# Inverting the triangular matrices of a delta-rule recurrence with 64x64 instead of 32x32 products, with read-out and preparation rearranged

## The chip, the cores and the metric

One core of one Trainium2 chip runs the whole program. The metric is device time in microseconds (us) of one execution; fewer is better.

## The reference

The program is a multi-block network on 512 latent and 256 context tokens. The change touches its recurrent mixer (twelve heads of 64, two directions), here cut to that:

```python
def rwkv_prepare(p, mu, w0, w2, a0, a2, g2, k_k, k_a):
    ...
    logw = -jax.nn.softplus(-(w0 + jnp.einsum('btdr,drc->btdc', jnp.tanh(wd), w2)).astype(f32)) - 0.5
    decay = jnp.exp(-jnp.exp(logw))
    a = jax.nn.sigmoid((a0 + jnp.einsum('btdr,drc->btdc', ad, a2)).astype(f32))
    g = jax.nn.sigmoid(gd) @ g2
    kk = (k * k_k).reshape(B, T, H_A, RWKV_HEAD)
    kk = kk / jnp.maximum(jnp.linalg.norm(kk, axis=-1, keepdims=True), 1e-12)
    kd = k[:, :, None, :] * (1.0 + (a - 1.0) * k_a)
    bd = kk.reshape(B, T, 1, D_A) * a
    ...
def wkv_scan(S0, r, w, k, v, kk, b, reverse):
    def step(S, inp):
        r_t, w_t, k_t, v_t, kk_t, b_t = inp
        sa = -jnp.einsum('bhij,bhj->bhi', S, kk_t)
        S = S * w_t[:, :, None, :] + sa[..., :, None] * b_t[:, :, None, :] + v_t[..., :, None] * k_t[:, :, None, :]
        return S, jnp.einsum('bhij,bhj->bhi', S, r_t)
    ...
def rwkv_readout(y, r, v, kd, g, r_k, lnx_g, lnx_b):
    mu = y.mean(-1, keepdims=True)
    var = jnp.mean(jnp.square(y - mu), -1, keepdims=True)
    yn = ((y - mu) * lax.rsqrt(var + GN_EPS)).reshape(B, T, D_A) * lnx_g + lnx_b
    coef = jnp.sum(r[:, :, None] * kd * r_k, axis=(2, 4))
    bonus = (coef[..., None] * v).reshape(B, T, D_A)
    return ((yn + bonus) * g).astype(g.dtype)
```

## The kernel before

The program is some twenty stages in a row; most multiply by streamed weights. The stage `rwkv_pairs` (L2240) runs the recurrence. It works on six pairs of heads (`PAIRS`), two heads filling the 128 partitions, and cuts the 768 tokens into twelve chunks (`NCH`) of 64 (`RC`). Within a chunk the recurrence is solved by the inverse of a 64x64 triangular matrix, made from products of keys; from chunk to chunk a 64x64 state is carried. The stage before it (`lora`, L1951) makes the inputs `wd`, `ad`, `gd` of the low-rank products.

Each engine has its instructions in the order in which they are written, and engines meet at semaphores. For `i` from -1 to 6 every engine runs `advance(i)`, then `recur(i)`:

- `advance(i)`, the *inversion phase*, does three jobs, interleaved by hand: it inverts the matrices of pair `i`, prepares pair `j = i+1`, and reads out pair `e = i-1`.
- `recur(i)`, the *recurrence phase*, takes twelve steps, each for both directions. It also makes the triangular matrices of pair `j` in twelve *units* (`turn_unit`, `triangle_unit`, and `triangles` on DVE), one to a step from the third step on, and the last two behind the steps. Before pair 0 the units stand alone: with the first preparation they make the stage's prologue.

**Inverting.** The matrices come in four groups (`COMBOS`: two directions, six chunks each). A 64x64 matrix is inverted by doubling: level 0 is identity minus the part next to the diagonal (POOL), levels 1 to 4 take the two diagonal 32-blocks up to their full size, and the join (`join_first`, `join_second`) adds the block between them. A level `l` of a group is a chain over four engines: POOL masks the matrix into `ct` (two buffers by `l % 2`); PE multiplies it by the inverse so far (`g_products`, L2403); ACT copies the product out of PSUM (`copy_g`, L2634); PE multiplies again (`u_products`, L2412); DVE subtracts that from `x` (`inverse`, L2808) and transposes it into `xd` (`turn_over`, L2802). Products are made by 32x32 quadrants of PE (`QUADS`), so that a 32-block is a matrix of its own; that is why `triangles` copies the diagonal 32-blocks once more, into `own` (L2929), and why the finished blocks and the join go into `xt`, by eight ACT copies (`copy_diagonal`, L2643) and eight on DVE (`join`).

**Preparing.** Per direction: `lora_decay` and `lora_rate`, fp32 products of 64 rows (L2378, `wide`); sigmoids (L2610, L2617); a scan and its centring (L2745); `linear_rate` (L2622) and `exponentials` (L2625, L2627); products for rates, query, receptance and updates on DVE. Each change between sigmoid and exponential loads a table on ACT.

**Reading.** `copy_y` (L2648), `mean` (PE, L2378 with `bones`), `centre_y` (DVE), `square_y` (L2652), `variance`, `root_y` (L2656), `invert_root` (L2826), `spread_root` (L2091), `scale_y` (L2830), `affine_y`, then `coefficients`, `bonus`, `add_bonus`, `gate` and `gate_y`. Before a recurrence starts to add up its outputs in PSUM, PE fills that area with zeros by a product (L2540).

## Time and profile before

| | before |
|---|---|
| median of 3 runs | 4580.6 us (4576.47 to 4582.39) |
| profiled execution | 4571.39 us, its span 4569.6 us |
| PE busy | 3924.0 us (86%) |
| PE weight loads | 3194.7 us (70%) |
| DVE busy | 1340.0 us (29%) |
| ACT busy | 1303.4 us (29%) |
| POOL busy | 1187.6 us (26%) |
| instructions | 86006 |

Busy times are shares of the span of the one profiled execution; engines overlap. The stage `rwkv_pairs` lies between about 2204 and 2962 us of that span: the prologue until 2276, then inversion and recurrence phases in turn, and at the end the read-out of the last pair. In the trace an fp32 product of PE is two records (an fp32r product is one), so a count there is twice the count of products in the code.

### The profile page before, as it was taken

Reading aid. Unit: us, or ns where it says so; the run is one execution under the profiler, and the core shown is the slowest. Engines: PE = TensorE matmul, PEld = TensorE weight load, DVE = VectorE, ACT = ScalarE, POOL = GpSimd, SP = SyncE. Lnnn points to the kernel's source line nnn. Section 1 sums busy time; section 2 is a strip of 40 time slices with the busy share of each in tenths; the row PEclk is TensorE's granted clock in tenths of the full one; section 3 lists DMA queues with packets and bytes.
Section 4 is the critical chain, followed back from the end, with each engine's and each line's share of the span. In section 5 each row is a group of like instructions: output and inputs, shape, how many; then the busy total and the mean of one; then the engine's idle time right before and its main releaser. Section 6 shows DMA issues by size and latency. Waiting matters only on the chain. (4 is left out here: it accounts for less than half of the span.)

```text
span 4569.6 us, 86006 instructions
## 1 busy us (share of the span) xinstructions
PE 3924.0 (86%) x36748; PEld 3194.7 (70%) x36748; DVE 1340.0 (29%) x2838; ACT 1303.4 (29%) x2196; POOL 1187.6 (26%) x665
## 2 busy tenths in 40 slices
PE   6798699999798899769588787678999969997997
PEld 4676588888576677658466666567888848765885
DVE  1327211111344211155455555331111130352111
ACT  0315321111354322232233333222112132453222
POOL 0311222222233333222111100112222213453442
PEclk8899899999899899989777777699999989998999
DMA  7210132232200435222200000003323202111221
...
DMA packets 120335, 343.82 MB, mean 75 GB/s; under 512 B 35551, under 2 KB 41567, under 8 KB 119647
## 3 DMA queue, kind: packets, MB, share of 16 engines
...
q14 instruction: 67, 0.55, 0.0%
...
## 5 line engine op out<-in xcount | busy, mean ns | idle before, releaser
L204 POOL TENSOR_TENSOR feed_low<-ring,feed_high 128x1024 fp32r<-128x1024 f32 (+1 forms) x240 | 626.8, 2612 | 1310.8 <-ACT feed_high L197 1310.8
L221 PE MATMUL ps<-hn_high,feed_high 128*128 128x512 f32 (+1 forms) x2112 | 758.1, 359 | 129.4 <-POOL feed_low L204 124.3
L221 PE MATMUL ps<-hn_low,feed_high 128*128 128x512 f32 (+1 forms) x2112 | 751.6, 356 | 0.0
L221 PE MATMUL ps<-hn_high,feed_low 128*128 128x512 f32 (+1 forms) x2112 | 750.5, 355 | 0.0
L221 PEld LDWEIGHTS ps<-hn_high,feed_high 128*128 128x128 f32 x2112 | 401.6, 190 | 214.9 <-issue 151.8
L221 PEld LDWEIGHTS ps<-hn_high,feed_low 128*128 128x128 f32 x2112 | 401.1, 190 | 56.8
L221 PEld LDWEIGHTS ps<-hn_low,feed_high 128*128 128x128 f32 x2112 | 401.8, 190 | 55.1
L197 ACT ACTIVATE feed_high<-ring 128x1024 fp32r<-128x1024 f32 (+1 forms) x240 | 272.9, 1138 | 487.3 <-PE ps L221 485.9
L1089 DVE TENSOR_TENSOR ps<-feed_gate,ps 128x768 f32<-128x768 f32 (+1 forms) x88 | 73.0, 830 | 1077.5 <-PE ps L221 1077.5
L221 PE MATMUL ps<-feed_hid_high,feed_high 128*128 128x512 f32 (+1 forms) x1056 | 377.6, 358 | 5.3 <-DVE feed_hid_low L1092 5.3
L221 PE MATMUL ps<-feed_hid_low,feed_high 128*128 128x512 f32 (+1 forms) x1056 | 377.2, 357 | 0.0
L221 PE MATMUL ps<-feed_hid_high,feed_low 128*128 128x512 f32 (+1 forms) x1056 | 376.5, 356 | 0.0
L221 PEld LDWEIGHTS ps<-feed_hid_high,feed_high 128*128 128x128 f32 x1056 | 201.7, 191 | 34.7 <-issue 6.1
L221 PEld LDWEIGHTS ps<-feed_hid_high,feed_low 128*128 128x128 f32 x1056 | 201.6, 191 | 28.6
L221 PEld LDWEIGHTS ps<-feed_hid_low,feed_high 128*128 128x128 f32 x1056 | 201.5, 191 | 28.0
L1052 ACT ACTIVATE feed_hid_high<-ps 128x768 f32 (+3 forms) x88 | 62.1, 705 | 551.1 <-DVE ps L1089 551.1
L1058 ACT ACTIVATE feed_gate<-ps 128x768 f32<-128x768 f32 (+1 forms) x88 | 62.0, 705 | 497.1 <-PE ps L221 497.1
L951 DVE SCALAR_TENSOR_TENSOR h<-ps,mod_even,h 128x512 f32 x96 | 54.8, 613 | 453.6 <-PE ps L221 453.6
L221 PE MATMUL ps<-project_mixed_high,project_high 128*128 128x512 f32 (+1 forms) x384 | 141.4, 368 | 26.6 <-DVE project_mixed_low L935 26.6
L2361 POOL TENSOR_TENSOR rwkv_ct<-rwkv_own,rwkv_level_mask 128x192 f32<-128x192 f32 x24 | 14.2, 592 | 520.5 <-DVE rwkv_own L2929 520.5
L204 POOL TENSOR_TENSOR project_low<-ring,project_high 128x1024 fp32r<-128x1024 f32 x32 | 78.5, 2455 | 243.8 <-ACT project_high L197 243.7
L221 PE MATMUL ps<-project_mixed_low,project_high 128*128 128x512 f32 (+1 forms) x384 | 140.0, 365 | 0.0
...
## 6 DMA issues: line engine op xcount, KB each, us to landing
...
```

Of the source, the lines that this page charges most:

```text
L197: act.activation(self.high[:, j % self.slots, 0:w], feed.ring[:, slot, 0:w], ACT.Copy).then_inc(self.high_ready, 1)
L204: pool.tensor_tensor(self.low[:, j % self.slots, 0:w], feed.ring[:, slot, 0:w], self.high[:, j % self.slots, 0:w].bitcast(F32), ALU.subtra ...
L221: mm = pe.matmul(dst, weights[a], values[b], start=first and n == 0, stop=last and n == 2)
L951: ins = dve.scalar_tensor_tensor(out=hs, in0=region(k, r)[:, a:b], scalar=k.mod[:, bass.ds(n + gate_at * KC, 1), s], in1=hs, op0=ALU.mult, ...
L1052: act.activation(hid[0][:, bass.ds(n, 1), :].rearrange("p a t -> p (a t)"), whole, ACT.Copy).then_inc(hid_high_ready, 1)
L1058: act.activation(gate, GATE, ACT.Silu).then_inc(gated, 1)
L1089: dve.tensor_tensor(whole, gate, UPR, ALU.mult).then_inc(multiplied, 1)
L2361: pool.tensor_tensor(ct[:, d, 0, gs, :], own[:, d, gs, :], levels[:, d, 0, :].unsqueeze(1).to_broadcast([P, GR, 32]), ALU.mult)
```

## The change

- **Levels.** A level now takes both 32-blocks of a 64x64 matrix in one product: weights of 64 columns and 32 streamed ones on two halves of PE, in place of 32 and 16 on four quadrants. POOL masks the full 64x64 matrix straight from `lt`, with one buffer `ct`, so a mask waits for the product that last read it. `own` and `xt` go; the join writes into `xd`, half of it on ACT and half on DVE. Level 0 of groups 0 and 1 and the level-1 masks of these are made in the recurrence before; groups 2 and 3 have their level 0 on DVE, at the start of `advance`.
- **Centring.** The values are multiplied by identity minus 1/64 as they are turned, so that outputs come out centred; `mean` and `centre_y` go.
- **Low-rank products** take split operands: high and low parts in fp32r, three products in place of one fp32 product. The `lora` stage makes `wide_high` and `wide_low`; ACT and POOL split the weights of the next pair in the recurrence. The reciprocal root is split likewise for `spread_root`, and the zero fill is an fp32r product.
- **Sigmoid** is 0.5 tanh(0.5 x + 0.5 b) + 0.5: a tanh and a scaled copy.
- **GpSimd** takes `rates` and `add_bonus` from DVE. The stage's constants come by fewer DMAs.
- The order within `advance` is another on every engine.

```diff
     act.activation(gd, gd, ACT.Sigmoid)
+    act.drain()
+    act.activation(wide_high[:, 0, :], wd, ACT.Copy).then_inc(high_ready, 1)
...
+    for n, m in enumerate((1, 0)):
+        dve.wait_ge(high_ready, n + 1)
+        dve.tensor_tensor(wide_low[:, m, :], inputs[:, m, :], wide_high[:, m, :].bitcast(F32), ALU.subtract)
...
-    for dst, name in ((ident2, "ident2"), (lmask, "tri_mask")):
-        sp.dma_start(dst[:], k.io[name]).then_inc(S["constants"], 16)
-    for q, qs in enumerate(QUADS):
-        cols = slice(32 * (q % 2), 32 * (q % 2) + 32)
-        sp.dma_start(ident32[qs, :], k.io["ident2"][qs, cols]).then_inc(S["constants"], 16)
-        sp.dma_start(levels[qs, :, :, :], k.io["level_mask"][qs, :, 0:JOIN, cols]).then_inc(S["constants"], 16)
+    sp.dma_start(ident2[:], k.io["ident2"]).then_inc(S["constants"], 16)
+    sp.dma_start(lmask[:, :, :], k.io["tri_mask"][:, :, 0:2 * RC]).then_inc(S["constants"], 16)
+    sp.dma_start(levels[:, :, :, :], k.io["level_mask"][:, :, 0:JOIN, :]).then_inc(S["constants"], 16)
...
+    def level_mask(i, l, c):
+        d, gs = COMBOS[c]
+        if l == 1 and c > 1:
+            pool.wait_ge(S["x_ready"], 20 * i + c + 1)
+        if l > 1:
+            pool.wait_ge(S["g_done"], 20 * i + 4 * (l - 2) + c + 1)
+        return pool.tensor_tensor(ct[:, d, gs, :], lt[d][:, gs, 0, :],
+                                  levels[:, d, l, :].unsqueeze(1).to_broadcast([P, GR, RC]), ALU.mult)
+
+    def rates(j, d):
+        pool.wait_ge(S["lin_ready"], 2 * j + d + 1)
+        pool.wait_ge(S["landed"], 48 * (j + 1))
+        if d == 0:
+            if j > 0:
+                pool.wait_ge(S["prep_done"], j)
+            pool.tensor_tensor(chunked(kds[:, j % 3, :]), decay, chunked(key), ALU.mult).then_inc(S["decay_free"], 1)
+        else:
+            pool.tensor_tensor(decay, decay, chunked(key), ALU.mult)
+        pool.tensor_tensor(a, a, unit, ALU.mult).then_inc(S["rates_done"], 1)
...
+            rates(j, 0)
+        if inverting:
+            for l in (3, 4):
+                for c in range(4):
...
+                if i >= 0:
+                    pool.wait_ge(S["sa_done"], 24 * i + 12)
+                pool.wait_ge(S["lt_ready"], 12 * j + 4 + c + 1)
+                level_mask(j, 0, c)
+                pool.drain()
+                pool.tensor_tensor(xd[:, d, gs, :], ident2[:, :].unsqueeze(1).to_broadcast([P, GR, RC]), ct[:, d, gs, :],
+                                   ALU.subtract).then_inc(S["xd_first"], 1)
             pool.drain()
...
+            for c in range(2):
+                level_mask(j, 1, c).then_inc(S["ct_ready"], 1)
...
-    def wide(dst, weights, src):
+    def wide(dst, parts):
+
         for a_, b_, _ in spans(TOK):
-            mm = pe.matmul(dst[:, a_:b_], weights, src[:, a_:b_], start=True, stop=True)
+            for n, (weights, values) in enumerate(parts):
+                mm = pe.matmul(dst[:, a_:b_], weights, values[:, a_:b_], start=n == 0, stop=n == len(parts) - 1)
...
+    def low_rank(dst, high, low, rows, m):
+        return wide(dst, ((high, wide_high[rows, m, :]), (high, wide_low[rows, m, :]), (low, wide_high[rows, m, :])))
...
+            for hs in HALVES:
+                mm = pe.matmul(k.ps[hs, c, 32 * m:32 * m + 32].rearrange("p (b w) -> p b w", w=2 ** l),
+                               ct[hs, d, n, :], one(x[hs, d, n, :], l, d), start=True, stop=True)
...
+            for hs in HALVES:
+                mm = pe.matmul(k.ps[hs, c, 32 * (GR + m):32 * (GR + m) + 32], xd[hs, d, n, :], g[hs, d, n, :],
                                start=True, stop=True)
...
-    def variance(e):
-        pe.wait_ge(S["ysq_ready"], e + 1)
         sums.quarters(pe, 4, t1).then_inc(S["var_done"], 1)
...
+        for q in range(4):
+            dst = k.ps[:, 4 + q // 2, QT * (q % 2):QT * (q % 2 + 1)]
+            pe.matmul(dst, pick_r[:, q, :], root_high[:, :], start=True, stop=False)
+            mm = pe.matmul(dst, pick_r[:, q, :], root_low[:, :], start=False, stop=True)
...
         if preparing:
             lora_decay(j, 0)
-        if reading:
-            mean(e)
         for l in range(1, JOIN):
             if inverting:
-                for c in range(4):
-                    g_products(i, l, c)
+                g_products(i, l, 0)
+                g_products(i, l, 1)
+            if reading and l == 1:
+                variance(e)
+            if inverting:
+                g_products(i, l, 2)
+                g_products(i, l, 3)
+            if preparing and l == 1:
+                lora_rate(j, 0)
+            if preparing and l == 3:
+                lora_decay(j, 1)
+            if reading and l == 4:
...
-                mm = pe.matmul(k.ps[hs, 7, m * RC:(m + 1) * RC], val[hs, j % 2, n * RC:(n + 1) * RC], ident2[hs, :],
+                mm = pe.matmul(k.ps[hs, 7, m * RC:(m + 1) * RC], val[hs, j % 2, n * RC:(n + 1) * RC], centre2[hs, :],
...
-                pe.matmul(R2[:, a_:b_], zeros[:, :], wd[:, a_:b_], start=True, stop=False)
+                pe.matmul(R2[:, a_:b_], blank[:, :], wide_high[:, 0, a_:b_], start=True, stop=False)
...
+        act.activation(decay, chunked(R3), ACT.Tanh, scale=0.5, bias=half_bias(j, d))
+        act.drain()
+        act.activation(decay, decay, ACT.Copy, scale=0.5, bias=0.5).then_inc(S["decay_ready"], 1)
+
...
-        act.activation(a, R3, ACT.Sigmoid, bias=p(j, f"a0_{d}")).then_inc(S["a_ready"], 1)
+        act.activation(a, R3, ACT.Tanh, scale=0.5, bias=half_bias(j, 2 + d)).then_inc(S["a_ready"], 1)
...
+        act.drain()
+        act.activation(a, a, ACT.Copy, scale=0.5, bias=0.5)
...
-    def copy_diagonal(i, d):
-        for q, qs in enumerate(QUADS):
-            ins = act.activation(xt[qs, d, :, 32 * (q % 2):32 * (q % 2) + 32], xd[qs, d, :, :], ACT.Copy)
-        ins.then_inc(S["xt_diagonal"], 1)
...
+    def join(i, c):
+        d, gs = COMBOS[c]
+        act.wait_ge(S["u_done"], 20 * i + 16 + c + 1)
+        for h in range(2):
+            qs = QUADS[2 * h + d]
+            ins = act.activation(xd[qs, d, gs, 32 - 32 * d:64 - 32 * d], k.ps[qs, c, GR * 32:GR * 64].rearrange("p (n c) -> p n c", c=32),
+                                 ACT.Copy, scale=-1.0)
+        ins.then_inc(S["join_odd"], 1)
...
+    def square_y(e):
         act.wait_ge(S["y_done"], e + 1)
+        act.activation(t1[:, :], R2, ACT.Square)
         act.activation(k.mo[:, e, :], R2, ACT.Copy).then_inc(S["y_copied"], 1)
...
-    def rates(j, d):
-        dve.wait_ge(S["lin_ready"], 2 * j + d + 1)
-        dve.wait_ge(S["landed"], 48 * (j + 1))
...
+    def first_level(i, c):
         d, gs = COMBOS[c]
...
+        dve.tensor_tensor(ct[:, d, gs, :], lt[d][:, gs, 0, :], levels[:, d, 0, :].unsqueeze(1).to_broadcast([P, GR, RC]), ALU.mult)
+        dve.drain()
+        dve.tensor_tensor(xd[:, d, gs, :], ident2[:, :].unsqueeze(1).to_broadcast([P, GR, RC]), ct[:, d, gs, :], ALU.subtract)
...
-        dve.tensor_tensor(xs, xs, packed(k.ps[:, c, GR * 16:GR * 32], l), ALU.subtract)
-        turn_over(i, l, c)
+        dve.tensor_tensor(xs, xs, packed(k.ps[:, c, GR * 32:GR * 64], l), ALU.subtract)
+        dve.drain()
+        dve.transpose(flat(xd[:, d, gs, :]), flat(x[:, d, gs, :])).then_inc(S["x_ready"], 1)
...
-    def centre_y(e):
-        dve.wait_ge(S["mean_done"], e + 1)
-        dve.scalar_tensor_tensor(out=k.mo[:, e, :], in0=R2, scalar=-1.0 / HEAD, in1=k.mo[:, e, :],
-                                 op0=ALU.mult, op1=ALU.add).then_inc(S["centred"], 1)
...
-        dve.reciprocal(root[:, :], root[:, :]).then_inc(S["rec_ready"], 1)
+        dve.reciprocal(root[:, :], root[:, :])
+        dve.drain()
+        dve.tensor_scalar(root_high[:, :], root[:, :], 1.0, None, ALU.mult)
+        dve.drain()
+        dve.tensor_tensor(root_low[:, :], root[:, :], root_high[:, :].bitcast(F32), ALU.subtract).then_inc(S["rec_ready"], 1)
...
-        for q, qs in enumerate(QUADS):
-            cols = slice(32 * (q % 2), 32 * (q % 2) + 32)
-            ins = dve.tensor_tensor(own[qs, d, 2 * u:2 * u + 2, :], k.ps[qs, 6, :].rearrange("p (n w) -> p n w", n=2)[:, :, cols],
-                                    lmask[qs, d, cols].unsqueeze(1).to_broadcast([32, 2, 32]), ALU.mult)
-        ins.then_inc(S["lt_ready"], 1)
+        dve.tensor_tensor(lt[d][:, 2 * u:2 * u + 2, :, :].rearrange("p n j c -> p (n j c)").rearrange("p (m w) -> p m w", m=4),
+                          k.ps[:, 6, :].rearrange("p (m w) -> p m w", m=4),
+                          lmask[:, d, :].unsqueeze(1).to_broadcast([P, 4, 2 * RC]), ALU.mult).then_inc(S["lt_ready"], 1)
```

PE in `advance(1)` (inverting pair 1, preparing pair 2, reading pair 0), from the first low-rank product to the second products of level 1. Before:

```order
L2378 MATMUL ps<-lora,rwkv_lora_weights 128x512
L2378 MATMUL ps<-lora,rwkv_lora_weights 128x256
L2378 MATMUL ps<-mo,rwkv_bones 128x512
L2378 MATMUL ps<-mo,rwkv_bones 128x256
L2403 MATMUL ps<-rwkv_x,rwkv_ct 32x16 x96
L2412 MATMUL ps<-rwkv_g,rwkv_xd 32x16 x48
```

And now:

```order
L2447 MATMUL ps<-lora_high,rwkv_wa_high 128x512
L2447 MATMUL ps<-lora_low,rwkv_wa_high 128x512
L2447 MATMUL ps<-lora_high,rwkv_wa_low 128x512
L2447 MATMUL ps<-lora_high,rwkv_wa_high 128x256
L2447 MATMUL ps<-lora_low,rwkv_wa_high 128x256
L2447 MATMUL ps<-lora_high,rwkv_wa_low 128x256
L2475 MATMUL ps<-rwkv_x,rwkv_ct 64x32 x24
L2094 MATMUL ps<-rwkv_t,rwkv_bones 32x192 x4
L2475 MATMUL ps<-rwkv_x,rwkv_ct 64x32 x24
```

The mean product is gone, the variance moved up between the groups of level 1, and a level's first product is 48 instructions in place of 96.

POOL for one pair. Before:

```order
L2361 TENSOR_TENSOR rwkv_ct<-rwkv_own,rwkv_level_mask 128x192
L2364 TENSOR_TENSOR rwkv_xd<-rwkv_ident,rwkv_ct 128x192
L2371 TENSOR_TENSOR rwkv_ct<-rwkv_own,rwkv_level_mask 128x192 x16
L2361 TENSOR_TENSOR rwkv_ct<-rwkv_own,rwkv_level_mask 128x192
L2364 TENSOR_TENSOR rwkv_xd<-rwkv_ident,rwkv_ct 128x192
```

The first two rows come four times before the third, which is four levels of four masks; the last two begin the next pair. And now:

```order
L2377 TENSOR_TENSOR rwkv_ct<-h,rwkv_level_masks 128x384
L2426 TENSOR_TENSOR rwkv_xd<-rwkv_ident,rwkv_ct 128x384
L2377 TENSOR_TENSOR rwkv_ct<-h,rwkv_level_masks 128x384
L2426 TENSOR_TENSOR rwkv_xd<-rwkv_ident,rwkv_ct 128x384
L2377 TENSOR_TENSOR rwkv_ct<-h,rwkv_level_masks 128x384 x2
L2369 TENSOR_TENSOR rwkv_wa_low<-rwkv_lora_weights,rwkv_wa_high 128x256
L2377 TENSOR_TENSOR rwkv_ct<-h,rwkv_level_masks 128x384 x6
L2386 TENSOR_TENSOR rwkv_kds<-ring 128x768
L2389 TENSOR_TENSOR ring<-ring 128x768
L2377 TENSOR_TENSOR rwkv_ct<-h,rwkv_level_masks 128x384 x8
L2388 TENSOR_TENSOR ring<-ring 128x12x64
L2389 TENSOR_TENSOR ring<-ring 128x768
```

The masks have twice the columns (`h` is the memory of `lt`), and the products for the rates (L2386 to L2389) stand among them, two of the four ahead of the masks of levels 3 and 4. The first six rows are now reached within the recurrence before.

## Rows read from the trace of the kernel before

**Rows 1.** Stretches: length, busy of PE, PEld, DVE, ACT, POOL, clock, DMA, GB/s

```profile
2276.00:2330.60 54.60, 41.47 (x1750) 32.10 (x1750) 28.03 (x64) 21.31 (x41) 13.81 (x18) 0.50 0.03 5
...
2378.50:2448.90 70.40, 51.40 (x1778) 36.18 (x1778) 33.46 (x69) 24.88 (x45) 11.64 (x18) 0.55 0.09 16
2448.90:2497.20 48.30, 43.57 (x1185) 41.42 (x1185) 32.19 (x113) 15.96 (x64) 3.55 (x7) 0.99 0.10 31
2855.80:2913.80 58.00, 37.40 (x1756) 30.02 (x1756) 19.89 (x55) 12.96 (x32) 10.15 (x18) 0.59 0.02 4
2942.00:2961.00 19.00, 10.87 (x28) 5.61 (x28) 6.13 (x6) 3.04 (x4) 0.00 (x0) 0.66 0.00 0
```

**Rows 2.** Timeline of PE in the inversion phase of pair 1: start, length, operation

```profile
2389.44 2.93 PE L2378 MATMUL ps<-lora,rwkv_lora_weights 64*128 64x512 f32 x4
...
2406.44 2.92 PE L2091 MATMUL ps<-rwkv_root,rwkv_pick 128*128 128x192 f32 x8 [2.23 <-DVE rwkv_root L2826]
...
2412.15 2.75 PE L2403 MATMUL ps<-rwkv_x,rwkv_ct 32*32 32x16 f32 x192
2414.73 0.90 PE L2412 MATMUL ps<-rwkv_g,rwkv_xd 32*32 32x16 f32 x50
...
2445.99 2.93 PE L2540 MATMUL ps<-lora,rwkv_zeros 128*128 128x512 f32 x4
```

**Rows 3.** Timeline of PE in the prologue, 64x64 products

```profile
2243.64 0.45 PE L2516 MATMUL ps<-rwkv_ident,rwkv_bb 64*64 64x64 f32 x4
2243.85 0.45 PE L2516 MATMUL ps<-rwkv_ident,rwkv_kb 64*64 64x64 f32 x4
...
2247.30 0.28 PE L2516 MATMUL ps<-rwkv_ident,rwkv_kb 64*64 64x64 f32 x4
2247.42 0.28 PE L2516 MATMUL ps<-rwkv_ident,rwkv_bb 64*64 64x64 f32 x4
```

**Rows 4.** Timeline of PE in the stage before, fp32r products

```profile
2000.15 0.39 PE L221 MATMUL ps<-hn_low,lora_high 128*128 128x512 f32 x1
2000.37 0.39 PE L221 MATMUL ps<-hn_high,lora_low 128*128 128x512 f32 x1
```

**Rows 5.** Groups of DVE by shape, 2277 to 2960: busy, mean ns, idle before

```profile
L2802 DVE STREAM_TRANSPOSE rwkv_xd<-rwkv_x 128x192 f32<-128x192 f32 x96 | 36.3, 379 | 7.3
L2808 DVE TENSOR_TENSOR rwkv_x<-rwkv_x,ps 128x96 f32<-128x96 f32 x96 | 23.7, 247 | 178.6 <-PE ps L2412 178.5
L2745 DVE TENSOR_TENSOR_SCAN ring<-rwkv_within,ring 128x780 f32<-128x780 f32 x10 | 18.9, 1893 | 11.3 <-ACT ring L2610 10.8
...
L2830 DVE TENSOR_TENSOR mo<-mo,ps 128x768 f32<-128x768 f32 x6 | 5.5, 923 | 3.0 <-PE ps L2091 3.0
```

**Rows 6.** Groups of POOL by shape: masks of levels, and a 768-column subtraction elsewhere

```profile
L2371 POOL TENSOR_TENSOR rwkv_ct<-rwkv_own,rwkv_level_mask 128x192 f32<-128x192 f32 x96 | 63.5, 689 | 52.8 <-PE ps L2403 51.2 <-issue 1.0
...
L649 POOL TENSOR_TENSOR hn_low<-affine_whole,hn_high 128x768 fp32r<-128x768 f32 x12 | 21.7, 1812 | 182.8 <-ACT hn_high L645 182.8
```

**Rows 7.** Groups of ACT by shape, 2277 to 2960

```profile
L2643 ACT ACTIVATE rwkv_xt<-rwkv_xd 32x384 f32<-32x384 f32 x48 | 24.9, 518 | 0.6
L2625 ACT ACT_TABLE_LOAD x10 | 12.8, 1283 | 0.2
```

**Rows 8.** Stretches for PE alone: busy, clock, DMA share, GB/s

```profile
2242.00:2244.00 2.00, 2.00 (x28) 0.50 0.04 8
2250.00:2252.00 2.00, 0.84 (x24) 1.00 0.83 299
2290.00:2292.00 2.00, 2.00 (x165) 0.50 0.03 8
```

**Rows 9.** Timeline of DVE, last units of pair 1's recurrence

```profile
2490.17 0.69 DVE L2924 TENSOR_TENSOR h<-ps,rwkv_tri_mask 128x512 f32<-128x512 f32 x1 [1.25 <-PE ps L2528]
2490.78 0.91 DVE L2929 TENSOR_TENSOR rwkv_own<-ps,rwkv_tri_mask 32x64 f32<-32x64 f32 x4
2492.88 0.69 DVE L2924 TENSOR_TENSOR h<-ps,rwkv_tri_mask 128x512 f32<-128x512 f32 x1 [1.19 <-PE ps L2528]
```

350 lines of the change are left out of this document (183 added, 167 removed).

## The prediction

> **What bounds the kernel now.** I read the views from the outside in. The page's first part makes TensorE (PE) the busy engine, but its share is an average over twenty stages. The change touches one of them, the recurrent stage (`rwkv_pairs`), and prepares its inputs one stage earlier. So I cut that stage with the stretches view [rows 1]. Each of the six head pairs passes an *inversion phase* (PE, VectorE (DVE), ScalarE (ACT) and GpSimd (POOL) take turns) and a *recurrence phase* of twelve steps. A full inversion phase takes 70.4 us and PE is busy for 51.4 us of it; a recurrence takes 48.3 us, PE busy for 43.6. The granted clock differs just as much: 0.55 against 0.99, so the inversion phase runs mostly at TensorE's lower level, 1.2 GHz, and the recurrence at 2.4 GHz. Neither phase is bound by one engine's throughput. The timeline of the inversion phase shows PE going from group to group [rows 2] with holes of 1.5 to 4 us, in which ACT copies a product out of PSUM or DVE subtracts and transposes.
>
> **The change, part by part.** All of it is costed against the profiled execution: 4571.4 us, span 4569.6, which is 9.2 us under the median 4580.6.
>
> *PE, level products.* Of each of four levels, 192 + 192 quadrant instructions, counted as the records of the trace (32 weight columns, 16 streamed), become 96 + 96 half instructions (64 weight columns, 32 streamed). At the lower clock the quadrant group takes 2414.73 - 2412.15 = 2.58 us for 192, 13.4 ns each [rows 2]; four quadrants run side by side, so one takes 54 ns. A half product with 64 weight columns and 64 streamed takes 0.21/4 = 53 ns at 1.2 GHz and 0.12/4 = 29 ns at 2.4 GHz [rows 3]; two halves run side by side, so one takes 106 ns. A quadrant product costs half of that: it follows the weight columns (32 of 64), not the streamed ones (16 of 64). So I price a new one by its 64 weight columns: 96 x 53 ns = 5.1 us per group at 1.2 GHz, 96 x 29 ns = 2.8 us at 2.4 GHz. The other bound, streamed columns alone, is half of each. Eight groups: 40.8 us or 22.3 us, against about 19 us in the phase before. At an equal clock the PE loses here.
> The Trainium skill ("TensorE: Matmul & The Clock Gate", section "LDWEIGHTS") gives a weight load as P/1.2 ns, P being columns; that is 53 ns for 64 columns and 27 ns for each of two side by side, at either clock. By it the low-clock group would take 2.6 us, and all of the low-clock case below would fall onto the high-clock one. The row of the 1.2 GHz product, 53 ns for each of two, does not agree, so I keep the row.
>
> *PE, wide products.* The four low-rank products go from fp32 at 2.9 us (1.2 GHz) [rows 2] to three fp32r passes. At 2.4 GHz such a pass takes 0.22 us for 512 columns [rows 4], 0.33 for the 768 here, so three are 1.0 us, and 2.0 at 1.2 GHz. The mean product (2.9) goes. Spreading the root falls from 2.9 to 1.3, the zero fill before the recurrence from 2.9 to 0.7. Coefficients and gate stay (2.9 each).
>
> *PE, sum of an inversion phase.* At 1.2 GHz: 40.8 + 4 x 2.0 + 5.8 + 0.8 (variance) + 1.3 + 4.1 (join) + 0.7 = 61.5 us. At 2.4 GHz: 32.8.
>
> *DVE.* A level step was 0.25 + 0.38 us, 0.64 from one to the next [rows 5]. Twice the columns at about 1 ns each (from 96 to 768 columns an operation goes from 0.25 to 0.92 [rows 5]) make 0.94; 16 of them are 15.0. First level: four operations of 0.54 and two transposes, 3.4. Scans 3.8 [rows 5], centring 2.0, root with its split 2.0, scale, bonus and gate 2.8, query to updates 4.1, half of the join 1.5: 34.6 us busy. GpSimd takes over 3.7 us of rates, and its masks double from 0.69 us to between 1.0 and 1.4 each [rows 6].
>
> *ACT.* Two of four table loads of 1.28 us per phase go [rows 7], and so do the eight copies into `xt` (0.52 us each [rows 7]); two 0.85 us copies come in behind each tanh pair. They lie beside PE work, except the copies before the join.
>
> *What the path becomes.* If the clock were high throughout, PE's 32.8 us would lie under a chain that DVE sets: its 34.6 us plus what it waits where a level's last product must cross PE. These waits are 2.5 before the first level, 1.6 after it, 0.3 at the second scan, 3.8 behind gate and rate product before level 4, 1.4 at the join and 1.8 for handoffs: 11.4, in all **46 us**. If it stayed low, PE is the chain: 61.5 and 2.5 for handoffs, **64 us**. Which one? In the windows of the prologue [rows 8], half products alone took the clock from 0.50 to 1.00 and kept it there while PE was busy for only 0.84 us of 2. The quadrant products of today sit at 0.50 with PE full. The new phase has half products everywhere, but still holes of about 2 us (behind the root, before level 4). I take 53 us, some 60% of the way from low to high.
>
> *Sum, against 4571.4.* Pairs 1 to 4: 70.4 or a little more, to 53, four times 17.4 = 69.6 saved. Pair 0 (54.6 us, no reading part): bounds 38 and 56, 45 taken, 9.5 saved. Pair 5 (58.0, nothing prepared): bounds 35 and 56, 43 taken, 15 saved. Triangles: four small DVE operations (0.91 us) leave each unit. Inside a recurrence that is free, since DVE idles there; in the last units of each, 2.71 us apart because PE waits for DVE [rows 9], it is on the path: 2.3 x 5 = 11.5. The prologue has twelve such units, 10 us, and 2.5 us in its chain of preparation, where four table loads (5.1) leave and tanh copies, weight split and GpSimd rates (0.9 us slower per operation [rows 5, 6]) enter. Last readout [rows 1]: mean and centring out, root split in, 3. The stage before gains two ACT and two DVE operations, which lie beside the pooling chain: 0. Together 121 us, giving 4450 for the profiled execution, 9.2 more for the median: **4460 us**.
>
> **The rivals.**
> 1. *Clock high throughout.* For: the prologue's windows. Against: holes of 2 us, after which today's phase is always back at 0.50. Savings 12.5 + 16.6 + 4 x 24.4 + 23 + 11.5 + 3 = 164; median 4416. Chance 0.15.
> 2. *Clock low throughout the inversion.* Then pair 0 loses 1.4, pairs 1 to 4 gain 6.4 each, pair 5 gains 2: 12.5 - 1.4 + 25.6 + 2 + 11.5 + 3 = 53; median 4527. Chance 0.10.
> 3. *GpSimd becomes the wait.* `ct` has one buffer now, so the mask of a level starts when the last level's first product is done, and the level-3 masks stand behind two rates of 1.81 us that wait for ACT. At 1.4 us a mask, four masks per level are 5.6 us where a level of my chain has 9 to 12; only the rates push, some 5 us a pair. That gives 58 a phase, median 4485. Chance 0.08. The Trainium skill ("GPSIMD Engine Reference", section "Engine selection") says elementwise work with two inputs belongs on VectorE, being about twice as slow here; 1.81 against 0.92 us agrees.
> 4. *Slower: the recurrence loses its clock.* Today the 2.9 us zero fill runs right before each recurrence [rows 2], and the clock is up when the steps begin. The change cuts it to 0.7 us. If 64-column products could not lift the clock by themselves, 43.6 us of busy PE would double: five recurrences 35 us longer each and the last 25, 200 us lost against 121 gained, median 4660. It decides when the low clock lasts for over 0.6 of every recurrence. Against it: the prologue lifts the clock on just such products [rows 8]. Chance 0.05, with mixed forms of it.
> 5. *DVE and GpSimd slow each other* until the gain is eaten. Today a 192-column mask takes 0.69 us on average with DVE busy beside it and 1.81 us is the price of 768 columns [rows 6], about what size alone explains, so little is lost there. No change then; chance 0.02.
>
> **How the numbers follow.** Forecast 0.60, rivals as above; 4460 is the likeliest case, a phase of 53 us, own range 4440 to 4490. The range runs from rival 1 to rival 2: 4415 to 4527, leaving out the slower cases and the tails. A difference under 0.2% (9 us) cannot be told from none by this measurement. Faster is the sum of the forecast and rivals 1 to 3, 0.93; the same is rival 5, 0.02; slower is rival 4, 0.05.
>
> **What would show it.** In the stretches of the changed kernel: phases of pairs 1 to 4 at 48 to 58 us with a granted clock of 0.7 to 0.85; half groups of 24 instructions at 29 or 53 ns each, at 15 or 27 ns if I have mispriced weight columns (then another 10 to 20 us less at the low clock, all in all); recurrences still 46 to 49 us at 0.99; DVE about 34 us busy in a phase, GpSimd 25 to 30; the last units of a recurrence 1.8 us apart. I am wrong if the phase is above 60 us, if `ct` on GpSimd is what PE waits for most, or if a recurrence shows a clock under 0.9.

## The result and the profile after

The changed kernel takes **4496.9 us** (median of 4 runs, 4495.9 to 4509.1), beside 4578.5 us for the kernel before: a ratio of 0.983, with a 95% interval of 0.981 to 0.986. It is faster by 1.7%, some 80 us. The forecast was 4460 us (4415 to 4527), faster: the sign and the range hold, but a third of the forecast gain is missing (the profiled executions differ by 74.7 us; the sum said 121).

The page of the changed kernel, its span and its busy times:

```profile
span 4494.9 us, 76585 instructions
PE 3964.1 (88%) x32152; PEld 3289.1 (73%) x32152; DVE 1318.6 (29%) x2530; ACT 1291.9 (29%) x2185; POOL 1288.9 (29%) x677
```

Nine thousand instructions fewer, and PE busy 40 us *more* in a span 75 us shorter. The stretches view of the changed kernel, cut at the end of the last triangle and at the first product of a recurrence (stretch, length, busy of PE, PEld, DVE, ACT, POOL, clock, DMA share, GB/s): inversion phase of pair 0; phase and recurrence of pair 1; phases of pairs 4 and 5:

```profile
2265.60:2321.80 56.20, 53.80 (x986) 50.93 (x986) 32.60 (x58) 19.55 (x38) 24.78 (x18) 0.53 0.04 7
...
2368.30:2426.10 57.80, 53.57 (x1010) 47.48 (x1011) 36.45 (x63) 23.02 (x42) 25.53 (x19) 0.68 0.07 14
2426.10:2473.30 47.20, 44.86 (x1185) 42.71 (x1184) 25.56 (x65) 15.74 (x65) 6.79 (x7) 0.96 0.14 37
...
2684.70:2742.90 58.20, 56.05 (x1010) 49.62 (x1011) 36.49 (x64) 23.13 (x42) 25.52 (x19) 0.63 0.03 9
2790.30:2840.00 49.70, 46.04 (x963) 41.90 (x959) 24.85 (x53) 10.47 (x27) 15.54 (x15) 0.65 0.01 3
```

A full phase fell from 72 to 58 us. The same cut in the kernel before, which leaves the last unit's copies into `own` in the phase, gives 71.3, 72.9, 72.8 and 72.3 us for pairs 1 to 4; cut behind these copies, as in [rows 1], it gives 70.4, 72.1, 72.0 and 71.5. Now it is 57.8, 58.6, 58.4 and 58.2. PE stood idle for 19 to 20 us of a phase before and stands idle for 2 to 4 now: it is busy for 93 to 96% of it, at a mean clock of 0.63 to 0.68. This is no longer a chain of handoffs. By the first cut recurrences did not move (47 us before and now), pair 0 hardly (55.4 and 56.2), and the clock in a recurrence went from 0.99 or 1.00 to 0.96.

The timeline of PE in the phase of pair 1 of the changed kernel (start, length, operation, idle before) shows the prices and the holes:

```profile
2369.60 1.59 PE L2475 MATMUL ps<-rwkv_x,rwkv_ct 64*64 64x32 f32 x48
2371.12 0.53 PE L2094 MATMUL ps<-rwkv_t,rwkv_bones 128*32 128x192 f32 x8
2372.52 0.89 PE L2475 MATMUL ps<-rwkv_x,rwkv_ct 64*64 64x32 f32 x24 [0.87 <-POOL rwkv_ct L2377]
2374.94 1.25 PE L2475 MATMUL ps<-rwkv_x,rwkv_ct 64*64 64x32 f32 x24 [1.53 <-POOL rwkv_ct L2377]
...
2378.34 5.34 PE L2484 MATMUL ps<-rwkv_g,rwkv_xd 64*64 64x32 f32 x96
2383.48 5.32 PE L2475 MATMUL ps<-rwkv_x,rwkv_ct 64*64 64x32 f32 x96
...
2410.49 2.27 PE L2475 MATMUL ps<-rwkv_x,rwkv_ct 64*64 64x32 f32 x72
...
2425.10 1.01 PE L2616 MATMUL ps<-lora_high,rwkv_blank 128*128 128x512 f32 x2
```

A group of 96 records takes 5.3 us at the low clock, to the end of its last record; from its start to the next group's it is 2383.48 - 2378.34 = 5.14 us, 54 ns a record. At the high clock it is 2.27/72 = 32 ns. The prediction said 53 and 29. The stretches view of the same phase, cut where the clock changes, shows when PE had which:

```profile
2368.30:2375.20 6.90, 4.41 (x95) 3.64 (x96) 5.41 (x7) 2.51 (x5) 3.73 (x3) 1.00 0.01 2
2375.20:2409.30 34.10, 34.10 (x488) 30.94 (x484) 21.25 (x33) 12.87 (x20) 16.55 (x14) 0.50 0.01 2
2409.30:2423.00 13.70, 11.95 (x344) 10.36 (x343) 7.81 (x17) 5.77 (x11) 3.70 (x3) 1.00 0.21 45
2423.00:2429.90 6.90, 6.88 (x169) 6.34 (x171) 1.97 (x7) 2.75 (x11) 1.56 (x1) 0.51 0.20 26
2429.90:2433.00 3.10, 3.07 (x102) 2.94 (x100) 2.40 (x6) 1.38 (x5) 0.00 (x0) 1.00 0.25 32
```

PE works for 34 us without a pause at 0.50, gets 13.7 us of high clock, and falls back 3 us before the recurrence begins, which starts its first 4 us at the low clock. In the kernel before the mean over a whole recurrence was 0.99 [rows 1].

### The profile page after: what moved, and what is told of

Read it like the earlier page. It is cut to its first block and busy times, and to the rows that moved or that the text cites. A ratio compares the mean times of both kernels' runs of the same rounds, so it can differ in the third digit from the quotient of the medians.

```text
span 4494.9 us, 76585 instructions
## 1 busy us (share of the span) xinstructions
PE 3964.1 (88%) x32152; PEld 3289.1 (73%) x32152; DVE 1318.6 (29%) x2530; ACT 1291.9 (29%) x2185; POOL 1288.9 (29%) x677
## 5 line engine op out<-in xcount | busy, mean ns | idle before, releaser
L2377 POOL TENSOR_TENSOR rwkv_ct<-h,rwkv_level_masks 128x384 f32<-128x384 f32 x108 | 123.3, 1166 | 266.6 <-DVE h L3015 164.5
L221 PE MATMUL ps<-project_mixed_high,project_low 128*128 128x512 f32 (+1 forms) x384 | 139.7, 364 | 0.0
```

Of the source, the lines that this page charges most:

```text
L221: mm = pe.matmul(dst, weights[a], values[b], start=first and n == 0, stop=last and n == 2)
L2377: return pool.tensor_tensor(ct[:, d, gs, :], lt[d][:, gs, 0, :], levels[:, d, l, :].unsqueeze(1).to_broadcast([P, GR, RC]), ALU.mult)
```

## The experiments

Each kernel was run beside the kernel before on the same chip; ratios are to that kernel, and the changed kernel's own is 0.983 [0.981, 0.986]. Executions of one kernel spread by 3 to 25 us here, so the text below rests on the lengths of phases in the profiles, one execution of each kernel. "The changed kernel" is the base of all twelve edits.

**e2_quadrants: the title of the change undone.** Levels by quadrants again, all else kept.

```diff
-    for hs in HALVES:
-        mm = pe.matmul(k.ps[hs, c, 32 * (GR + m):32 * (GR + m) + 32], xd[hs, d, n, :], g[hs, d, n, :],
+    for q, qs in enumerate(QUADS):
+        b = q % 2
+        mm = pe.matmul(k.ps[qs, c, 32 * (GR + m) + 16 * b:32 * (GR + m) + 16 * b + 16], xd[qs, d, n, 32 * b:32 * b + 32],
+                       g[qs, d, n, 16 * b:16 * b + 16],
```

(the first products alike; GpSimd zeroes the off-diagonal blocks at the end of a phase.)

> Changed kernel, but the level products are made by 32x32 quadrants again (32 weight columns, 16 streamed), all else kept, and the off-diagonal blocks set to zero by GpSimd at the end. Theory A, the inversion phase is bound by PE, whose 64-column products are dear: a group at the low clock falls from 5.3 to 2.6 us, PE busy in a phase from 54 to about 35 us, and the phase of pairs 1 to 4 from 58 to 46 to 50 us; total 4430 to 4450. Rival B, a chain over DVE, ACT and GpSimd sets the phase and PE only fills it: phase 58 +- 1 us, total 4497 +- 6.

Measured: ratio 0.984 [0.982, 0.986], 4495 us, the same as the changed kernel, as rival B had it. Stretches of its phases of pairs 1, 2 and 3:

```profile
2368.40:2423.80 55.40, 42.99 (x1778) 35.66 (x1778) 35.63 (x64) 23.25 (x42) 27.98 (x23) 0.57 0.08 16
2470.80:2529.70 58.90, 44.70 (x1780) 37.02 (x1781) 36.14 (x64) 23.13 (x42) 28.20 (x23) 0.54 0.09 17
2576.60:2632.90 56.30, 43.31 (x1779) 35.86 (x1780) 36.71 (x64) 23.24 (x42) 28.20 (x23) 0.57 0.09 17
```

Some eleven us of PE work left a phase (pair 1: 53.6 to 43.0), and the phases of pairs 1 to 4 lost under two on average (55.4, 58.8, 56.2, 56.0). Neither theory holds as stated. PE was the bound, but right behind it lies the chain over the other engines: PE now stands idle for 12 to 14 us, among them these two waits in level 1, on the timeline of PE in the phase of pair 3:

```profile
2581.22 0.83 PE L2484 MATMUL ps<-rwkv_x,rwkv_ct 32*32 32x16 f32 x48 [1.76 <-POOL rwkv_ct L2377]
2583.64 0.84 PE L2484 MATMUL ps<-rwkv_x,rwkv_ct 32*32 32x16 f32 x48 [1.59 <-POOL rwkv_ct L2377]
```

And PE had less of the high clock (0.54 to 0.57 in place of 0.63 to 0.68), so that its other products took longer; why, no run shows. The 64x64 products by themselves are worth nothing here: pairs 0 to 4 are a little shorter with quadrants, pair 5 is 4 us longer (54.0).

This run also says where most of the gain is. With quadrants as in the kernel before, its phases are still 15 us shorter (56.6 us on average, 71.5 before, cut behind the copies): 8 us are PE work that is gone (51.4 to 43.4) and 7 us are idle time of PE (20.0 to 13.2). The work is mostly that of the wide products; by the prediction's prices at the low clock it is 4 x 0.9 + 2.9 + 1.6 + 2.2 = 10 us, an estimate. The shorter waits come of the other edits together (order, centring, copies into `xt`).

**e3_two_prices: what a small product costs.** Second products split in two, with the same result.

```diff
+    at = 32 * (GR + m)
+    if l == 1 or l == 3:
+        for b in range(2):
+            mm = pe.matmul(k.ps[hs, c, at + 16 * b:at + 16 * b + 16], xd[hs, d, n, :], g[hs, d, n, 16 * b:16 * b + 16],
+                           start=True, stop=True)
+    elif l == 2:
+        for b in range(2):
+            mm = pe.matmul(k.ps[hs.start + 32 * b:hs.start + 32 * b + 32, c, at:at + 32], xd[hs, d, n, 32 * b:32 * b + 32],
+                           g[hs, d, n, :], start=True, stop=True)
```

> Changed kernel, second products split in two with the same result: levels 1 and 3 as two products of 64 weight columns and 16 streamed ones, level 2 as two of 32 weight columns and 32 streamed ones; level 4 as it was. If the price follows weight columns: levels 1 and 3 10.6 us a group at the low clock in place of 5.3, level 2 still 5.3; a phase 8 to 11 us longer, total about 4555. If it follows streamed columns: levels 1 and 3 still 5.3, level 2 10.6; a phase 5 us longer, total about 4528.

Measured: ratio 1.000 [0.999, 1.001], 4572 us: all of the gain is gone. Timeline of PE in its phase of pair 0, groups at the low clock:

```profile
2280.92 10.44 PE L2487 MATMUL ps<-rwkv_g,rwkv_xd 64*64 64x16 f32 x192
2291.18 5.33 PE L2475 MATMUL ps<-rwkv_x,rwkv_ct 64*64 64x32 f32 x96
2296.44 3.05 PE L2491 MATMUL ps<-rwkv_g,rwkv_xd 64*32 64x32 f32 x192
...
2327.34 5.33 PE L2494 MATMUL ps<-rwkv_g,rwkv_xd 64*64 64x32 f32 x96
```

Half the streamed columns cost the same: (2291.18 - 2280.92)/192 = 53 ns a record for 16 columns as for 32, so the group doubled to 10.3 us. The price follows weight columns, as the prediction took it. For half the *weight* columns the expectation (still 5.3 us) was wrong: the same level product as two of 32 weight columns takes 3.05 us where one of 64 takes 5.33. The starts of the records in the trace say why. Records of 64 weight columns start in pairs, 107 ns from pair to pair. Those of 32 start four at a time (7, 6 and 7 ns apart, then 33 or 34), 53 to 59 ns from four to four, here and in the quadrant products of the kernel before. So half the weight columns cost about half, and twice as many products stand side by side. Phases of pairs 0 to 4 came out at 67 to 73 us.

**e4_lowrank_fp32.** One fp32 product for three fp32r ones; it leaves out the low parts.

```diff
-    return wide(dst, ((high, wide_high[rows, m, :]), (high, wide_low[rows, m, :]), (low, wide_high[rows, m, :])))
+    return wide(dst, ((high.bitcast(F32), wide_high[rows, m, :].bitcast(F32)),))
```

> Changed kernel, each low-rank product as one fp32 product of the high parts in place of three fp32r products (leaves out the low parts). Theory A, PE-bound phase: each product 2.9 us at the low clock in place of 1.9, so +3 to +4 us in each phase of pairs 0 to 4 and +4 us in the prologue: total 4513 to 4521. Rival B (a chain elsewhere sets the phase): phases within 1 us, only the prologue +4: 4501.

Measured: ratio 0.990 [0.987, 0.993]; profiled span 4516.7, 21.8 us over the changed kernel's. Phases of pairs 0 to 4: 58.2, 59.6, 58.8, 63.1, 66.4 (56.2, 57.8, 58.6, 58.4, 58.2 without the edit), 17 us together. The profiled execution (4518.5 us) is where the theory of a PE-bound phase put the total, the median (4525.6) 4 us above its range. Single phases are not there: they grew by 0.2 to 8.2 us, and the two that grew most, 13 of the 17 us, had a lower clock (0.61 and 0.55; 0.66 and 0.63 without the edit). The edit's own work and that of the clock are not told apart here.

**e5_rates_dve and e6_sigmoid: work off PE.** The rates back on DVE:

```diff
+    def rates(j, d):
+        dve.wait_ge(S["lin_ready"], 2 * j + d + 1)
+        dve.wait_ge(S["landed"], 48 * (j + 1))
+        dve.tensor_tensor(a, a, unit, ALU.mult)
...
     if reading:
         scale_y(e)
+    if preparing:
+        rates(j, 0)
```

> Changed kernel, the four rate products a pair back on DVE (query and updates wait for nothing else). Theory A', a phase is PE's work at the granted clock plus some 4 us of waits, so work elsewhere is free while DVE (36.5 us of 58 today, 40 then) keeps below: phases within 1 us, prologue -1 to +1, total 4491 to 4503. Rival, DVE's chain sets the phase: +4 us a phase, 4517.

Measured: ratio 0.983 [0.981, 0.984]; phases of pairs 1 to 4 58.7 to 59.1 us, DVE busy 39.3 to 39.6 us in one. And the sigmoids back:

```diff
-    act.activation(decay, chunked(R3), ACT.Tanh, scale=0.5, bias=half_bias(j, d))
-    act.drain()
-    act.activation(decay, decay, ACT.Copy, scale=0.5, bias=0.5).then_inc(S["decay_ready"], 1)
+    act.activation(decay, chunked(R3), ACT.Sigmoid, bias=p(j, f"w0_{d}")).then_inc(S["decay_ready"], 1)
```

> Changed kernel with the sigmoids of before: two more table loads of 1.28 us on ACT for each direction, two 0.85 us copies fewer. Theory A': phases within 1 us, the prologue (no PE work beside it) +1 to +3: total 4498 to 4504. Rival, ACT's table loads lie on the chain: +2 to +3 us in each of five phases as well, 4510 to 4514.

Measured: ratio 0.986 [0.984, 0.988]; phases of pairs 1 to 4 58.4 to 59.0 us, the prologue 1.9 us longer. Neither part of the change is worth more than 3 us. Work on DVE and ACT in a phase is covered by PE, as expected.

**e7_own_copies: the triangles.**

```diff
+    for q, qs in enumerate(QUADS):
+        cols = slice(32 * (q % 2), 32 * (q % 2) + 32)
+        ins = dve.tensor_tensor(own[qs, :, :], k.ps[qs, 6, :].rearrange("p (n w) -> p n w", n=2)[:, :, cols],
+                                lmask[qs, d, cols].unsqueeze(1).to_broadcast([32, 2, 32]), ALU.mult)
```

> Changed kernel, each triangle unit on DVE with its four small block copies again (into a scratch tile). They cost 0.83 us where PE waits for DVE: twelve units in the prologue, the last two of each of five recurrences: 10 + 5 x 1.65 = 18 us, total 4515. If my prediction's 2.3 us a recurrence were right, 21.5 us; if recurrence gained nothing, 10 us, 4507.

Measured: ratio 0.994 [0.992, 0.996], 4538 us: the dearest of the parts put back, 35 us by the profiled spans, twice the 18 expected. Timeline of DVE at the end of pair 1's recurrence, then at the end of the prologue:

```profile
2494.19 0.69 DVE L3016 TENSOR_TENSOR h<-ps,rwkv_tri_masks 128x512 f32<-128x512 f32 x1 [1.19 <-PE ps L2605]
2494.80 0.91 DVE L3021 TENSOR_TENSOR rwkv_own<-ps,rwkv_tri_masks 32x64 f32<-32x64 f32 x4
2496.90 0.69 DVE L3016 TENSOR_TENSOR h<-ps,rwkv_tri_masks 128x512 f32<-128x512 f32 x1 [1.19 <-PE ps L2605]
```

```profile
2279.34 0.69 DVE L3016 TENSOR_TENSOR h<-ps,rwkv_tri_masks 128x512 f32<-128x512 f32 x1 [2.08 <-PE ps L2605]
2279.95 0.91 DVE L3021 TENSOR_TENSOR rwkv_own<-ps,rwkv_tri_masks 32x64 f32<-32x64 f32 x4
2282.93 0.69 DVE L3016 TENSOR_TENSOR h<-ps,rwkv_tri_masks 128x512 f32<-128x512 f32 x1 [2.07 <-PE ps L2605]
```

In the recurrence the units stand 2.71 us apart, as in [rows 9]; the changed kernel's, without the copies, 1.89 us:

```profile
2470.68 0.69 DVE L3015 TENSOR_TENSOR h<-ps,rwkv_tri_masks 128x512 f32<-128x512 f32 x1 [1.19 <-PE ps L2604]
2472.57 0.69 DVE L3015 TENSOR_TENSOR h<-ps,rwkv_tri_masks 128x512 f32<-128x512 f32 x1 [1.19 <-PE ps L2604]
```

Counted to the end of the last unit's copies, recurrences are 49.7 to 51.1 us in place of 46.4 to 47.4: 16.6 us for the five, 3.3 each. That is four times the 0.83 us of a unit's copies: the last two units, the copies of the last one, and the fourth step, which takes 5.19 us in place of 4.36 and so waits for DVE as well. In the prologue the units stand 3.59 us apart, because there the clock never rose. Stretches of the prologue from 2230 to the last triangle, with the copies, without, and in the kernel before, which has the copies too:

```profile
2230.00:2283.60 53.60, 37.26 (x432) 34.05 (x432) 28.45 (x74) 10.16 (x20) 10.86 (x9) 0.50 0.19 46
```

```profile
2230.00:2265.60 35.60, 26.29 (x432) 23.76 (x432) 18.50 (x25) 9.26 (x20) 10.82 (x9) 0.73 0.23 62
```

```profile
2230.00:2275.20 45.20, 26.32 (x436) 22.41 (x436) 28.91 (x75) 11.68 (x20) 3.54 (x6) 0.84 0.22 53
```

The same 432 records, 18 us apart (18.8 to the end of the copies): 12 x 0.83 = 10 us are the copies, the rest goes with the clock, held at 0.50, though PE is busy for 70% of the time here and for 74% there. The copies by themselves do not keep the clock down: the kernel before has them, and its clock there is 0.84. What held it down in this run stays open. 18.8 and 16.6 make up the 35 us; the phases themselves did not change.

**e1_zero_fp32: does the fill warm the clock?**

```diff
-    pe.matmul(R2[:, a_:b_], blank[:, :], wide_high[:, 0, a_:b_], start=True, stop=False)
+    pe.matmul(R2[:, a_:b_], zeros[:, :], wide_high[:, 0, a_:b_].bitcast(F32), start=True, stop=False)
```

> Changed kernel with the fp32 zero fill of before (2.9 us at the low clock, now 1.0) ahead of each recurrence. Theory 'the fill warms the clock': the first step of a recurrence falls from 4.7 us to the 3.1 to 3.5 us of before and the clock of the first 4 us is 1.00; per pair +1.9 - 1.5, so the total stays within 4 us of 4497. Rival 'the fill is only time': first step stays at 4.7 us, six times +1.9 = 11 us, 4508.

Measured: ratio 0.989 [0.986, 0.991], 4518 us, more than either theory gave. The first step is 3.56 to 3.87 us in pairs 0 to 4 (4.04 to 5.04 in the changed kernel, 3.09 to 3.45 before), and recurrences shorten by 0.2 to 1.4 us, 0.9 on average. On the timeline of PE around the start of pair 1's recurrence:

```profile
2433.36 2.93 PE L2616 MATMUL ps<-lora_high,rwkv_zeros 128*128 128x512 f32 x4
2436.22 0.49 PE L2631 MATMUL ps<-rwkv_sm,rwkv_qq 64*64 64x64 f32 x4
...
2440.03 0.34 PE L2631 MATMUL ps<-rwkv_sm,rwkv_qq 64*64 64x64 f32 x4
```

So the longer fill takes 1.9 us and gives back 1: it covers a part of the low stretch that would else fall into the recurrence, and doesn't end it. It does not warm the clock. Of the 25 us between the profiled spans, six fills are 11. The phases of pairs 3 to 5 have more than their fill, 63.6, 62.9 and 57.7 us at 0.61, 0.58 and 0.53, and 6.6 us lie ahead of pair 0's phase, where the code is the same.

**e8_mean_product: centring undone.** Mean product and subtraction as in the kernel before, ACT and DVE in an order to match; the variance stands behind all four groups of level 1.

```diff
-    ... val[hs, j % 2, n * RC:(n + 1) * RC], centre2[hs, :],
+    ... val[hs, j % 2, n * RC:(n + 1) * RC], ident2[hs, :],
+    def mean(e):
+        pe.wait_ge(S["y_copied"], e + 1)
+        wide(R2, ((sums.bones[:, :], k.mo[:, e, :]),)).then_inc(S["mean_done"], 1)
```

> Changed kernel with the mean product of before (2.9 us at the low clock, 1.5 at the high) and its subtraction on DVE, values turned by the plain identity. Theory A': +1.5 to +3 us in each of the phases of pairs 1 to 5 and +3 in the last read-out: total 4508 to 4516. Rival, the mean lies in a hole of PE ahead of the level products: phases within 0.5 us, total 4500.

Measured: ratio 0.985 [0.982, 0.987]; but the phases of pairs 1 to 4 are 55.0 to 55.3 us, 3 us *shorter* with more to do, and pair 5's is 57.0 (49.7). The stretches view says why: the start of the phase of pair 1, the low stretch that follows, and pair 5's phase.

```profile
2371.30:2385.80 14.50, 13.01 (x288) 10.95 (x288) 11.85 (x17) 9.07 (x14) 7.27 (x6) 1.00 0.01 2
2385.80:2409.70 23.90, 22.25 (x296) 19.71 (x298) 16.34 (x25) 7.16 (x13) 13.02 (x10) 0.50 0.01 2
2781.50:2838.60 57.10, 55.11 (x991) 49.49 (x990) 25.78 (x54) 11.35 (x28) 15.53 (x15) 0.53 0.01 3
```

The high clock lasted for 14.5 us from the start of the phase in place of 6.9, and pair 5 had next to none of it. The 12 us that four phases gained are not in the total: 7 went in pair 5's phase, some 4 in the last read-out, which has the product too, and 7 in the stages behind it, where the code is the same. What kept the clock up became the question of the last four runs.

**e9_mask_early and e10_dve_order.** Take away the two holes of 0.87 and 1.53 us behind `ct`, then those behind DVE.

```diff
-        if l == 1 and c > 1:
-            pool.wait_ge(S["x_ready"], 20 * i + c + 1)
+        if l == 1 and c > 1 and i > 0:
+            pool.wait_ge(S["g_done"], 20 * i)
...
-        dve.tensor_tensor(ct[:, d, gs, :], lt[d][:, gs, 0, :], levels[:, d, 0, :]...
+        dve.tensor_tensor(xd[:, d, gs, :], lt[d][:, gs, 0, :], levels[:, d, 0, :]...
```

> Changed kernel, but DVE makes level 0 of groups 2 and 3 in place in xd, without ct, so that GpSimd's level-1 masks of these groups need not wait for DVE. Theory C, the holes of 0.87 and 1.53 us in which PE waits for these masks early in a phase let the clock fall 10 us sooner than a PE without them (e8_mean_product, whose extra product covers them, has phases of 55.1 us in place of 58.2 with 2.9 us more PE work): holes gone, clock at 1.00 until at least 15 us into the phase, PE busy under 50 us, phases of pairs 1 to 4 at 52 to 55 us, total 4468 to 4485. Rival, the holes are only 2.4 us of time: phases 56 us, total 4487 to 4490, clock falling where it does now. Rival 2, GpSimd takes the next place (its masks of level 2 come late): phases unchanged.

and for e10_dve_order also:

```diff
+        inverse(i, 1, 0)
+        inverse(i, 1, 1)
+        inverse(i, 1, 2)
+        inverse(i, 1, 3)
     if preparing:
         centre(j, 0)
     if reading:
         invert_root(e)
```

> As e9_mask_early, and on DVE the centring of the scan and the reciprocal root stand behind all four subtractions of level 1, not between them. At the high clock of e8_mean_product PE waited 0.95 and 2.03 us for these in level 2. Theory C: these holes shrink to under 1 us together and the clock stays high longer still: phases 2 to 4 us under those of e9_mask_early. Rival: the waits move to level 2's later groups, phases within 1 us of e9_mask_early.

Measured: ratios 0.986 [0.983, 0.989] and 0.985 [0.983, 0.988], no gain. In e9_mask_early the holes behind GpSimd are gone (one of 1.34 us behind DVE's transposes is left), and the clock falls when it did. Stretches of its phases of pairs 1 to 4:

```profile
2363.30:2418.30 55.00, 51.85 (x1010) 46.19 (x1010) 37.52 (x63) 23.04 (x42) 24.76 (x18) 0.69 0.07 14
2465.30:2526.40 61.10, 58.94 (x1011) 51.97 (x1012) 37.57 (x64) 23.03 (x42) 24.12 (x18) 0.59 0.07 14
2573.90:2633.10 59.20, 54.60 (x1012) 48.56 (x1013) 38.32 (x64) 23.03 (x42) 23.99 (x18) 0.66 0.07 14
2680.20:2743.60 63.40, 61.98 (x1010) 55.31 (x1010) 37.87 (x63) 23.47 (x42) 24.16 (x18) 0.54 0.03 9
```

The same code in the same order, four times within one execution, takes 55 to 63 us, and the clock's mean runs the other way, 0.69 to 0.54. Most of this scatter is whether the 13.7 us of high clock late in a phase are granted (pairs 1 and 3), half granted (pair 2) or not at all (pair 4). Theory C falls. e10_dve_order gave 63.3, 60.9, 59.1 and 63.4 us.

**e11_wide_filler and e12_half_filler.** PE work that nobody needs, ahead of the holes, in pairs 1 to 4: the mean product alone, or the first products of two groups made twice.

```diff
+    if inverting and preparing and reading:
+        pe.wait_ge(S["y_copied"], e + 1)
+        wide(R2, ((sums.bones[:, :], k.mo[:, e, :]),))
```

```diff
+    for again in range(2 if l == 1 and c < 2 and 0 < i < PAIRS - 1 else 1):
         for m, n in enumerate(range(gs.start, gs.stop)):
```

> Changed kernel; in the phases of pairs 1 to 4 PE also makes the mean product of before (128 rows, 768 streamed columns, fp32), whose result nobody reads, right behind the first low-rank product. It tells whether e8_mean_product's phases of 55.1 us came of that product or of its other edits. Theory D, this product itself keeps the clock up: clock at 1.00 for about 14 us from the start of a phase in place of 7, phases of pairs 1 to 4 55 to 56 us, total 8 to 12 us under the changed kernel (ratio to before about 0.981). Rival, it is only work: +1.5 us at the high clock, phases 59 to 60 us, ratio about 0.985.

> Changed kernel; in the same four phases PE makes the first products of groups 0 and 1 of level 1 twice (48 half products more, 1.5 us at the high clock, about the time of the wide filler). Theory D1, a wide product keeps the clock up and half products of 32 streamed columns don't: clock falls where it does now, about 7 us into the phase, phases 58 to 60 us, ratio about 0.985. Theory D2, any PE work ahead of the holes keeps it up: as e11_wide_filler, phases 55 to 56 us.

Measured: ratios 0.986 [0.984, 0.987] and 0.987 [0.985, 0.988]. Phases 63.3, 57.8, 61.0, 56.3 and 63.9, 57.9, 57.9, 63.5 us. Two stretches of e11_wide_filler, the phases of pairs 1 and 4, and the start of the latter until the clock falls:

```profile
2370.60:2433.90 63.30, 62.20 (x1014) 54.69 (x1015) 36.80 (x63) 23.70 (x42) 25.57 (x19) 0.56 0.08 15
...
2694.00:2750.30 56.30, 53.48 (x1014) 46.91 (x1015) 36.46 (x63) 23.26 (x42) 25.56 (x19) 0.70 0.03 10
2694.00:2702.60 8.60, 7.53 (x120) 5.80 (x120) 5.41 (x7) 3.75 (x7) 5.44 (x5) 1.00 0.01 2
```

With either filler the high clock at the start of a phase lasts 7 to 9 us. That is longer than in the changed kernel (6.9, 4.4, 4.5 and 1.2 us in pairs 1 to 4), but far from the 14.5 of e8_mean_product, and no phase is shorter than the 55.0 to 55.3 there. So the mean product alone is not what did it, and theory D falls in both forms. What in that kernel kept the clock up for longer, four times in a row, stays open; the variance's place and the order on ACT and DVE were not tried apart. No version beat the changed kernel clearly; e5_rates_dve (4491.5) and e2_quadrants (4494.6) are level with it.

## Why the prediction was right, and where it was not

**The bound and the price of PE were right.** A low-clock group at 5.1 us measured 5.1 from start to start, and the low-clock phase of the second rival, 61.5 + 2.5 = 64 us, is close to what came out when the clock stayed low for all but its first 4.5 us: 63.4 us with 61.98 busy at 0.54 (pair 4 of e9_mask_early). Wholly low it would have been a few us longer (an estimate), so the sum was somewhat short: at the low clock a low-rank product takes 2.2 us for 2.0, spreading the root 2.0 for 1.3, the zero fill 1.0 for 0.7. Of the two prices weighed for 64 weight columns the row's stood: 54 ns at 1.2 GHz, 32 at 2.4. The Trainium skill ("TensorE: Matmul & The Clock Gate", section "LDWEIGHTS") gives a weight load as P/1.2 ns with no word on the clock; for two of 64 columns side by side that makes 27 ns each, an estimate from its figure. This trace comes near it at the high clock and does not agree with it at the low one. e3_two_prices confirms that weight columns set the price. GpSimd's masks (1.17 us on average, 1.0 to 1.4 forecast; 25.5 us of POOL in a phase, 25 to 30 forecast) and DVE (36.5 us, 34.6 forecast) were sized well too.

**The step that failed is "I take 53 us, some 60% of the way from low to high".** The phases of pairs 1 to 4 came to 58.2 us, at 0.63 to 0.68: about a third of the way. In the prediction's cut, behind the copies, pairs 1 to 4 saved 53 us where 70 was forecast. For pair 0 it failed altogether: 56.2 us at 0.53, the bound of the low case, where 45 was taken (11 us); pair 5 came to 49.7 for 43 (7 us). The choice was made from the prologue, where half products of 64 and 128 streamed columns had run at the high clock [rows 8]. In the new phase PE stood at 0.50 for 34 us without a pause. What sets the clock apart in the two places no run shows. Rows of the new product did not exist, and the nearest ones were not near enough; a forecast at the low case with the high one as a rival would have stood on the last row of [rows 8], where PE full of small products is at 0.50. That the total still fell into the range is owed to its width, which took in both clocks.

**One sign of being wrong did show.** What PE waits for most in a phase is `ct` on GpSimd: 2.4, 1.9 and 2.1 us in pairs 1 to 3 (0.3 in pair 4), about half of its idle time. It was little, and e9_mask_early, which takes these waits away, is no faster.

**The triangles were right in size and mostly taken back.** 2.3 us a recurrence was forecast; the last two units are 1.65 us shorter and the last one's own copies are gone, 2.5 together. e7_own_copies measures 3.3, since its fourth step waits for the copies as well: inside a recurrence they are not free, though the prediction took them so. But counted to the end of the copies the five recurrences shortened by 3.9 us only, for 11.5 forecast, since two things came in that the sum had at nothing. Their first step takes 4.7 us in place of 3.2 on average, at the low clock: a small form of the rival "the recurrence loses its clock". And the fourth step takes 4.36 us in place of 3.50, in pairs 0 to 4 alike, behind query and receptance products that DVE now makes in the second step. There PE waits for a triangle on DVE (timeline of PE, fourth step of pair 1):

```profile
2439.91 0.44 PE L2604 MATMUL ps<-rwkv_qq,rwkv_bb 64*64 64x128 f32 x4 [0.64 <-DVE h L3015]
```

With 0.4 us less in the second step, the last step begins 1.3 us later in pair 1 and 2.2 us in pair 2, against the 2.5 us gained behind it. The prediction gave the moved products no price because DVE idles in a recurrence; it idles for 4.5 us in the first step and for 1 to 2 us in each from the fifth on, but for 1 us or less in each step between.

**The prologue** gained 7.7 us of the 12.5 (6.9 to the last triangle), the stages ahead of the pairs 2.7 (forecast 0). From the last recurrence on the gain is 0.8 us (forecast 3).

**Table loads and rates** were put at next to nothing, as they are (e6_sigmoid +3 us, e5_rates_dve -4 by the profiled spans, both within the scatter). The rival "DVE and GpSimd slow each other" had a true core, see below. What it costs a phase no run measures; more work on DVE was covered there (e5_rates_dve).

**Where the gain lies.** By stretches the 75 us are 2.7 ahead of the pairs, 7.7 in the prologue, -1.7 in pair 0's phase, 53.0 in those of pairs 1 to 4, 8.3 in pair 5's, 3.9 in the recurrences and 0.8 behind. So 61 of 75 lie in phases that have PE idle for less and, by e2_quadrants, owe nothing on balance to the 64x64 products. Undoing single parts of the changed kernel costs 35 us for the copies into `own`, 22 for the split low-rank products (with the clock's part in it), 3 or less each for the sigmoid and the rates, and nothing for the 64x64 products. These prices do not add up to the gain: the 35 us lie in the prologue and the recurrences, where the kernel before, with the same copies, is only 12 us longer. The centring, the eight copies into `xt`, the order, the shorter root and fill were not tried apart, except centring, whose price was lost in the clock; how the 61 us divide among them and the low-rank products is not shown.
